# Boundary sums of split tiles on TensorE, a spread conditioning vector in the first stage, and an earlier value eviction in linear attention

## The reference, cut to what matters

```
mods = silu(c) @ w_ada + b_ada                 # shifts, scales, gates from one vector c of 1024
h = rmsnorm(x, g_pre) * (1 + sc) + sh
x = x + 0.5 * gt * rmsnorm(swiglu(h, w_gu, w_dn), g_post)     # first block, feed-forward
x = x + gt2 * rmsnorm(token_mixer(h, ...), g_post)            # first block, mixer
h = h + 0.5 * gt * swiglu(modulate(rmsnorm(h)), ...)          # second block: no norm on the way out
```

## Time and profile before

| | |
|---|---|
| median of three executions | 2604.65 us |
| the profiled execution | 2605.15 us, span 2603.4 us |
| PE busy | 2558.6 us (98% of the span) |
| PEld, DVE, ACT, POOL busy | 2095.1, 1116.4, 988.4, 1046.8 us |
| chain that ended last | PE 93%, DVE 4%, ACT 2%, issue 1% |

### The profile page before, as it was taken

How to read it: one execution, slowest core, us unless ns; L and a number is a source line. 1 busy time by engine, 2 the same in 40 slices (tenths; PEclk the granted TensorE clock), 3 DMA queues, 4 the chain that set the end, 5 groups by cost and what they waited for, 6 DMA issues and landing times.

```text
span 2603.4 us, 35693 instructions
## 1 busy us (share of the span) xinstructions
PE 2558.6 (98%) x12770; PEld 2095.1 (80%) x12770; DVE 1116.4 (43%) x2159; ACT 988.4 (38%) x1590; POOL 1046.8 (40%) x464
## 2 busy tenths in 40 slices
PE   6999999999999999999999999999999999999998
PEld 5888888888777888888889888889777678988887
DVE  7444336754444135644315543123544456322222
ACT  5222237444445334322334322233554344322221
POOL 0444454333323444544455444452222235244443
PEclk9999999999999999999999999999999999999999
DMA  7455532122222333455532554333112223223333
GB/s 293 150 192 192 184 130 75 61 71 85 85 91 79 105 97 122 159 193 192 181 122 79 198 193 145 104 122 104 49 56 76 82 78 113 65 97 97 97 105 97
DMA packets 78571, 313.72 MB, mean 121 GB/s; under 512 B 9072, under 2 KB 11888, under 8 KB 69008
## 3 DMA queue, kind: packets, MB, share of 16 engines
q1 hardware_dynamic: 65520, 238.61, 27.9%
q10 hardware_dynamic: 12960, 73.86, 8.0%
HBM read 310.31 MB, written 2.13 MB: 120 GB/s over the span
## 4 chain that ended last, share of the span: by engine, by line
PE 93%; DVE 4%; ACT 2%; issue 1%; DMA 0%; POOL 0%; DVEq 0%; ACTq 0%
PE bank L1929 26%; PE bank L1931 25%; PE bank L1930 25%; PE bank L1967 2%; PE bank L1968 2%; PE bank L1969 2%; PE pair L2178 1%; PE bank L2360 1%; PE pair L2250 1%; PE bank L2237 1%; PE pair L2388 1%; PE bank L2267 1%; PE bank L2368 1%; DVE xr L1275 0%; PE bank L2452 0%
## 5 line engine op out<-in xcount | busy, mean ns | idle before, releaser
L554 POOL TENSOR_TENSOR w_lo<-raw,w_hi 128x1024 fp32r<-128x1024 f32 x412 | 1008.3, 2450 | 1469.8 <-ACT w_hi L593 1469.8
L593 ACT ACTIVATE w_hi<-raw 128x1024 fp32r<-128x1024 f32 x420 | 443.8, 1059 | 1085.7 <-PE bank L1931 1035.4
L1929 PE MATMUL bank<-h_hi,w_hi 128*128 128x512 f32 x2064 | 825.4, 400 | 2.1 <-ACT vt L758 2.1
L1931 PE MATMUL bank<-h_hi,w_lo 128*128 128x512 f32 x2064 | 805.0, 390 | 0.0
L1930 PE MATMUL bank<-h_lo,w_hi 128*128 128x512 f32 x2064 | 804.2, 390 | 0.0
L1929 PEld LDWEIGHTS bank<-h_hi,w_hi 128*128 128x128 f32 x2064 | 388.1, 188 | 98.5 <-issue 19.2
L1931 PEld LDWEIGHTS bank<-h_hi,w_lo 128*128 128x128 f32 x2064 | 387.7, 188 | 82.6
L1930 PEld LDWEIGHTS bank<-h_lo,w_hi 128*128 128x128 f32 x2064 | 388.3, 188 | 79.8 <-issue 4.1
L1393 DVE TENSOR_TENSOR prod<-bank,rstd 128x512 f32<-128x512 f32 x87 | 60.2, 691 | 430.5 <-PE bank L1931 419.5
L1929 PE MATMUL bank<-act_hi,w_hi 128*128 128x512 f32 x616 | 239.6, 389 | 0.0
L1930 PE MATMUL bank<-act_lo,w_hi 128*128 128x512 f32 x616 | 239.6, 389 | 0.0
(11 more groups left out here) (439 smaller groups left out, 2994.4 us busy)
## 6 DMA issues: line engine op xcount, KB each, us to landing
raw<-slabs_dram SPq DMA_DIRECT2D x420, 512.0 KB, 3.5
adaw<-ada_dram ACTq DMA_DIRECT2D x62, 1024.0 KB, 6.8
ada<-ada_dram SPq DMA_DIRECT2D x8, 1024.0 KB, 20.3
x<-xt_dram SPq DMA_DIRECT2D x4, 512.0 KB, 8.2
adaw<-ada_dram SPq DMA_DIRECT2D x2, 1024.0 KB, 24.4
fneg<-fneg_scratch ACTq DMA_DIRECT2D x4, 512.0 KB, 3.7
sq<-fneg_scratch ACTq DMA_DIRECT2D x4, 512.0 KB, 3.6
w<-w_dram SPq DMA_DIRECT2D x1, 2048.0 KB, 8.0
```

Of the source, the lines that this page charges most:

```text
L554: nc.gpsimd.tensor_tensor(wl[s][:], raw[s][:], wh[s][:], ALU.subtract).then_inc(lo_done, 1)
L593: nc.scalar.activation(wh[s][:], raw[s][:], ACT.Copy).then_inc(hi_done, 1)
L1929: MM(out, wh[s][:, k], a, start=first and j == 0, stop=False)
L1931: ins = MM(out, wl[s][:, k], a, start=False, stop=end and j == len(tiles) - 1)
```

## The change: what it does

1. First stage. The broadcast transfer is gone. `c` comes as 8 columns of the small table `cols`; ACT takes silu of 128x8, PE turns each column into a row over all partitions with 8 matmuls against the identity into two PSUM banks, and DVE copies them to `silu_c`. The squares of x are shared: ACT the even tiles, DVE the odd ones. They are no longer added on DVE: PE sums each tile by itself, 32 one-column matmuls in place of 4. The load of ACT's root table moves ahead of the squares. DVE's list changes: both `mods` of tile 0 stand behind the reciprocal, and `mods(1)` ahead of slabs 4 and 5; ACT's high part of slab 5 moves behind h of tile 1; SP fetches slab 3 ahead of the second piece of modulation weights.
2. Boundaries. PE sums `ssacc`, `yyacc`, `xyacc` ahead of the split tiles (`sum_plain`), and then each split tile by itself (`sum_split`): `sq` against two columns (one and the gain's square), and the product `xr = 2 y x`, the only instruction that is left of four in `half_sums`, against ones. ACT squares first and then scales, and frees the bank. With one slab per tile (b = 2) `out_halves(1)` moves behind the first two tiles of `split_h`.
3. Linear attention. `gla_value(i + 1, 0)` moves to the end of `gla_exponentials(i + 1)`, ahead of the copies to `oa_hi`.

```diff
-            sp.dma_start(silu_c[:, 0], A["cvec"][0:1].to_broadcast([P, D])).then_inc(c_in, 16)
...
-            first_slabs(0, 1, 2)
+            first_slabs(0, 1, 2, 3)
             first_mods(1)
-            first_slabs(3, 4, 5)
+            first_slabs(4, 5)
...
+                    ins = nc.scalar.activation(y[:, t, hc], src, ACT.Identity, scale=post_g[:, t:t + 1])
+                ins.then_inc(acc_free[(m + PLAIN[b] + half) % 2], 1)
...
                     gla_exponentials(i + 1, range(4, len(LEVELS)))
+                    gla_value(c + 6, m + 6, i + 1, 0)
...
-            act.wait_ge(c_in, 16)
-            nc.scalar.activation(silu_c[:, 0], silu_c[:, 0], ACT.Silu).then_inc(silu_c_done, 1)
-            for n in range(KT):
+            act.wait_ge(cols_in, 16)
+            nc.scalar.activation(c_cols, c_cols, ACT.Silu).then_inc(silu_c_done, 1)
+            table(ACT.Sqrt)
+            for n in range(0, KT, 2):
                 act.wait_ge(x_in[n // 2], 16)
                 nc.scalar.activation(y[:, n], x[:, n], ACT.Square).then_inc(sx_done, 1)
-            table(ACT.Sqrt)
...
-                for c in {0: (2, 3, 4, 5), 4: (6,), 5: (7,)}.get(n, ()):
+                for c in {0: (2, 3, 4), 1: (5,), 4: (6,), 5: (7,)}.get(n, ()):
...
-                dve.wait_ge(ssadd, SSADD[b] + PLAIN[b])
-                for t in range(t0, KT):
-                    product = V.scalar_tensor_tensor(ST[:, hc], bk[:, halves(t - t0)], post_x[:, t:t + 1], x[:, t, hc], ALU.mult, ALU.mult)
...
-                    V.tensor_tensor(ssacc[:, hc], ssacc[:, hc], squared(t, half)[:, hc], ALU.add)
-                    V.scalar_tensor_tensor(yyacc[:, hc], squared(t, half)[:, hc], post_s[:, t:t + 1], yyacc[:, hc], ALU.mult, ALU.add)
...
-                    last = V.tensor_tensor(xyacc[:, hc], xyacc[:, hc], ST[:, hc], ALU.add)
+                    product = V.scalar_tensor_tensor(xr[:, t, hc], y[:, t, hc], 2.0, x[:, t, hc], ALU.mult, ALU.mult)
+                product.then_inc(half_summed, 1)
...
+            def sum_plain(b, half):
...
+                pe.wait_ge(ssadd, SSADD[b] + PLAIN[b])
+                for t in range(2):
+                    for q, a in enumerate((ssacc, yyacc, xyacc)):
+                        MM(at[:, 3 * t + q:3 * t + q + 1], a[:, t0 + P * t:t0 + P * (t + 1)], ones[:, 0:1], ...
+            def sum_split(b, half):
...
+                pe.wait_ge(half_summed, 2 * (b - 1) + half + 1)
+                for t in range(2):
+                    tokens = slice(t0 + P * t, t0 + P * (t + 1))
+                    for n in range(PLAIN[b], KT):
+                        MM(at[:, 3 * t:3 * t + 2], sq[:, n % 2, tokens], one_s[:, n], ...
+                        ins = MM(at[:, 3 * t + 2:3 * t + 3], xr[:, n, tokens], ones[:, 0:1], ...
...
-                                if half and done == (8 + 5 * (SPLIT[b] - 1) if TWO[b] else 6):
-                                    sum_out(b, 0)
+                                    if done == 1:
+                                        sum_plain(b, 0)
+                                    if done == 4 + SPLIT[b]:
+                                        sum_split(b, 0)
+                                    if done == 8 + SPLIT[b]:
+                                        spread(ev, 0, SC1, 0)
+                                    if done == 12 + SPLIT[b]:
+                                        spread(ev + 1, 4, SC1)
...
-                    in_step(0, 2, {2: lambda: sum_out(p, 1), ...
+                    in_step(0, 2, {1: lambda: sum_plain(p, 1), 2: lambda: sum_split(p, 1), ...
...
-            pe.wait_ge(x_sum, 1)
-            for t in range(TT):
-                ins = MM(ST[:, t:t + 1], ssacc[:, P * t:P * (t + 1)], ones[:, 0:1], start=True, stop=True)
+            pe.wait_ge(silu_c_done, 1)
+            pe.wait_ge(const_in, 32)
+            for j in range(KT):
+                ins = MM((SC0, OV)[j // 4][:, P * (j % 4):P * (j % 4 + 1)], c_cols[:, j:j + 1].to_broadcast([P, P]), ident[:], ...
+            for n in range(KT):
...
+                for t in range(TT):
+                    ins = MM(ST[:, t:t + 1], y[:, n, P * t:P * (t + 1)], ones[:, 0:1], ...
```

More of the change, by code:

```diff
@@ L218, in build @@
         ident = sb("ident", [P, P])
-        table = sb("cols", [P, NCOLS + 12])
-        cols, post_s, sx = table[:, 0:NCOLS], table[:, NCOLS:NCOLS + 8], table[:, NCOLS + 8:NCOLS + 12]
+        table = sb("cols", [P, NCOLS + 20])
+        cols, post_s, sx = table[:, 0:NCOLS], table[:, NCOLS:NCOLS + 16], table[:, NCOLS + 16:NCOLS + 20]
+        one_s = post_s.rearrange("p (t z) -> p t z", z=2)
+        c_cols = cols[:, COLS["c"]:COLS["c"] + KT]
         silu_at = cursor[0]
@@ L397, in scratch, with squared @@
             return (SC0, OV)[n % 2][:, 0:HALF]
-        def squared(t, half=0):
-            return sq[:, t % 2] if half else (SC0, OV)[t % 2][:]
+        def squared(t):
+            return (SC0, OV)[t % 2][:]
         def sums_at(half):
@@ L618, in std @@
                 act.wait_ge(s_sum, 2 * (b - 1) + half + 1)
-                at = sums_at(half) if TWO[b] else ST[:, 2 * half:2 * half + 2]
-                root(rcol[:, 2 * half:2 * half + 2], at[:, 0:2])
+                at = sums_at(half)[:, 0:6].rearrange("p (t q) -> p t q", q=3)[:, :, 0] if TWO[b] else ST[:, 2 * half:2 * half + 2]
+                root(rcol[:, 2 * half:2 * half + 2], at)
             def std_new(b, half):
@@ L795, in mix1 @@
                 for i in range(HG):
[L796 removed]
+                    gla_head(c + 6 * i, m + 6 * i, i, i < HG - 1, () if i == 0 else (1,))
                     if i == 1:
@@ L1240, in new_sum @@
                 dve.wait_ge(std_done, ev + 1)
-                V.tensor_copy(sums[:, 0:4], sums_at(half)[:, 2:6])
+                V.tensor_copy(sums[:, 0:4].rearrange("p (t q) -> p t q", q=2),
+                              sums_at(half)[:, 0:6].rearrange("p (t q) -> p t q", q=3)[:, :, 1:3])
                 recip(ev, c0)
@@ L1870, in h_low @@
                 V.tensor_tensor(hl[:, n], (SC0, OV)[n % 2][:], hh[:, n], ALU.subtract).then_inc(h_done, 2)
-            dve.wait_ge(sx_done, 2)
-            chain.link(V.tensor_tensor(ssacc[:], y[:, 0], y[:, 1], ALU.add))
-            for n in range(2, KT):
-                dve.wait_ge(sx_done, n + 1)
-                total = V.tensor_tensor(ssacc[:], ssacc[:], y[:, n], ALU.add)
-                if n < KT - 1:
-                    chain.link(total)
-            total.then_inc(x_sum, 1)
-            mods(0, 0)
+            for n in range(1, KT, 2):
+                dve.wait_ge(x_in[n // 2], 16)
+                V.tensor_tensor(y[:, n], x[:, n], x[:, n], ALU.mult).then_inc(x_sum, 1)
             dve.wait_ge(x_std, 1)
+            V.tensor_copy(silu_c[:, 0, 0:T], SC0)
+            chain.link(V.tensor_copy(silu_c[:, 0, T:D], OV[:]))
+            dve.wait_ge(x_std, 2)
             V.tensor_copy(sx[:], ST[:, 0:TT])
             V.reciprocal(rcol[:, 0:TT], rcol[:, 0:TT]).then_inc(x_std, 1)
+            mods(0, 0)
             mods(0, 1)
             set_pre(0)
-            dve.wait_ge(x_std, 4)
+            dve.wait_ge(x_std, 5)
             scaled_x(0)
@@ L1891, in _ @@
             h_low(0)
-            for c in range(2, AHEAD):
-                low(c)
+            low(2)
+            low(3)
             for z in range(2):
@@ L1896, in _ @@
             set_pre(1)
-            for n in range(1, KT - 1):
+            low(4)
+            low(5)
+            h_low(1)
+            scaled_x(2)
+            for z in range(2):
+                mods(2, z)
+            set_pre(2)
+            for n in range(2, KT - 1):
                 scaled_x(n + 1)
@@ L1994, in out_tiles @@
                                     ins.then_inc(slab_done, 1)
-                                if half and done == (8 + 5 * (SPLIT[b] - 1) if TWO[b] else 6):
+                                if half and TWO[b]:
+                                    if done == 1:
[6 more added lines that the diff above has]
+                                        spread(ev + 1, 4, SC1)
+                                elif half and done == 6:
                                     sum_out(b, 0)
-                                if half and done == (11 + 5 * (SPLIT[b] - 1) if TWO[b] else 9):
-                                    spread(ev, 0, SC1, 0 if TWO[b] else HALF)
-                                if half and TWO[b] and per > 1 and done == 17:
-                                    spread(ev + 1, 4, SC1)
+                                elif half and done == 9:
+                                    spread(ev, 0, SC1, HALF)
                     if half == 0:
                         ins.then_inc(half_done, 1)
-                if TWO[b] and per == 1:
-                    spread(ev + 1, 4, SC1)
-                elif b == LAST:
+                if b == LAST:
                     sum_out(b, 1)
```

75 lines of the change are left out of this document (37 added, 38 removed).

## The result

The changed kernel takes 2609.49 us, median of 19 executions (2607.65 to 2613.86); the kernel before took 2605.69 beside it (2604.45 to 2607.26, 19 executions). The ratio is 1.0016, with a 95% interval of 1.0009 to 1.0022: slower by 2.3 to 5.7 us. The profiled execution is one of the longest, 2613.31 us with a span of 2611.5.

A forecast was written before the change was run, and what follows sets the result against it. PE was taken to bound the kernel, busy 2558.6 of 2603.4 us. First stage +10.8, boundaries -2.0 and +0.9, linear attention -2.2 sum to +7.5: a median of 2612, range 2603.5 to 2617 (forecast's own 2608.5 to 2616).

The forecast's parts named there:

- First stage, +10.8: Up to the first head's end: PE's sums end 9.7 us later, DVE's wait costs 1.1; bounds +4.5 and +10.8.
- I take the first: First-stage sums: all 64 records at 0.21 us, 13.5 us (+9.7), chosen over all at 0.11, 7.2 us (+3.4).
- the rival of the clock that rises in the start, for a part of the sums: First-stage sums half at each clock level: they take 10.4 us, the whole change costs +4.4, 2609; chance 15%.
- the two such rivals: Clock up for all first-stage sums (whole change +1.2, 2606; 18%) or for half of them (+4.4, 2609; 15%).
- The argument from the earlier trace: First stage: PE's sums and spread before (14.65 to 19.25 us) did not bring the upper clock; used against its rise.
- Boundary after mixer 1, -2.0: Boundary with two split tiles: gain 3.6 us at the upper clock, less a clock charge; bounds -3.6 and +1.
- the charge of 1.6 for the clock: Boundary after mixer 1: 1.6 us set against the 3.6 gain for a possible stretch at the lower clock.
- Boundaries after feed-forward 0 and 1, +0.9: Both boundaries with one split tile: +0.9 us together, head's half 0 ending 0.4 sooner in each; bounds -0.8 and +3.6.
- another 0.85 for each: Boundaries after feed-forward 0 and 1: half of 1.7 us each, in case longer small sums let the clock fall.
- Linear attention, -2.2: Earlier value tile copy removes PE's three waits of 0.7 us each: -2.2 us, bounds -2.1 and -2.6.

The follow-up runs named there:

- packed kernel: The changed kernel with its table of columns packed into 1024 bytes, so tensors behind it keep the addresses of before: 2607.02 us, ratio 1.0006 to the kernel before.

## Why the prediction was right, and where not

The forecast was 2612.0 and the time 2609.5, slower as forecast and inside the range. But the nearness of the sum of +7.5 to the measured +4.2 is in part luck, since errors cancel. By ratios of the single parts, each uncertain by 2.4: first stage +5.7, boundaries -2.1, value tile -3.4, and +4.7 that no step had: together +4.9.

- **First stage, +10.8.** For the profiled execution every term was near: start of PE 7.4 and not 8.7 (`wa` landed sooner), sums 13.65 against 13.5, `xr` 8.1 later against 9.7, DVE's gap 1.48 against 1.5, +9.99 in all at 67 us against 10.8. The first head took 1.9 of that, not 1.1. For the median it failed at "I take the first", all sums at 0.21. The packed kernel's sums took 10.55 us, with the clock up for their first part, and the stage costs 5.7. This was the rival of the clock that rises in the start, for a part of the sums (10.4 us, 15%); the two such rivals got 33% together, and 11 of 19 executions have the mean clock that goes with it. The eight spread matmuls with the sums right behind them were weighed too lightly. The argument from the earlier trace rows, that the sums and spread before did not bring the upper level, was drawn from four sums and four spread matmuls with a pause of 0.73 between them, not from eight in a row with sums at once behind them.
- **Boundary after mixer 1, -2.0.** First h 0.8 sooner in the trace (+7.22 at 978, +6.41 at 1028.67) against 0.7; POOL's waits in the boundary are down from 3.8 to 1.9. Where the clock holds, 3.1 were gained against 3.6; in the changed kernel's trace, where it fell, 1.1. The 2.0 between them stand against the charge of 1.6 for the clock.
- **Boundaries after feed-forward 0 and 1, +0.9.** Wrong in sign. Without a low stretch the second gave -0.6 against -0.4. I charged another 0.85 for each in case the clock falls further, and in the changed kernel's trace it did not. The first came to -2.7 in the trace of the changed kernel, where half of the low stretch of before was missing. That half is no gain of the change: the kernel with the value tile alone had 3.41 us of it, and the one with shifted slab buffers none from 400 to 440 us, both with the old boundary:

```profile
400.00:440.00 40.00, 39.08 (x254) 33.86 (x253) 22.14 (x55) 31.25 (x53) 20.43 (x17) 1.00 0.15 46
```

- **Linear attention, -2.2.** The trace has -2.5, made of -3.0 for the three waits and +0.6 for the wait for `qc`, which does not come from this part. The size of the term was low: the three waits were read from their rows as 0.7 each, and each took 1.0 from PE.
- **What was missing.** The edit `NCOLS + 20` was taken as storage without a price. At 4.7 us it is the largest single cost beside the first stage, and it hid what the first stage, the boundaries and the value tile did better than forecast.

## What to carry to other kernels

A change to one small table can move every tensor that is laid out behind it; look at the addresses before pricing the instructions, and run the old kernel with the same shift, as here, to see what the shift alone costs. A wait that is listed for PE costs more than its row says; compare start to start with the regular spacing. A profile is one execution: before a wait or a low stretch is credited to an edit, look whether kernels without the edit have it too. And an engine that waits is not free for any work: here TensorE loaded 128 columns of weights for one column of result, and 28 such matmuls cost more than the seven adds of DVE that they replaced.

## What the runs showed of the hardware

- Matmuls of 512 columns whose weights, or whose moving tiles, start 64 bytes off a multiple of 128, counted from the kernel's first tensor in SBUF, come 228.9 (moving tile) to 232.3 ns (weights, 60 to 72 us) apart on average, 226.7 otherwise. In this kernel, with PE busy for 98% of its time, that was 4.7 us in 2606. Why the chip does so, and what other shifts would do, no run here shows.
- The Trainium skill, "TensorE: Matmul & The Clock Gate", Part 1, has the clock throttled by default and released by activity. That agrees with the start here: the upper level came around the end of the eight spread matmuls in the packed kernel, and with the 14 dummy ones it was there by 7.81 us. That it can be lost again while PE is busy all the time, in one-column sums (12 to 20 us, 0.50 granted with PE busy 3.00 of 3.00), is shown by these rows.
- The executions of the changed kernel fall into two groups, and the longer ones have the higher mean granted clock (0.996 to 0.999 against 0.993 to 0.995). The sign is not general: with the 14 dummy matmuls the four longest executions have the lower mean (0.990 to 0.992 against 0.994 and 0.995). So the mean alone does not tell what an execution did. Whoever reads one profile reads one of these cases: the profiled execution of the changed kernel was 3.8 us above its median.
